# A two-block network on one core: order of the summed feed-forward products, and the gated recurrence with its two directions' scores added before they are multiplied

## The chip, the cores and the metric

The kernel runs on one core of a Trainium2 chip. A core has five engines that run their own instruction lists and meet at semaphores: TensorE (matrix products, PE in the rows, its weight loads PEld), VectorE (DVE), ScalarE (ACT), GpSimd (POOL) and SyncE (SP), which here only issues the weight transfers. The metric is the time of one execution on the device in microseconds (us); the time before is the median of three, 3287.19 us (3286.39 to 3287.36).

## The reference

Two blocks follow each other on 256 tokens of width 2048. The first has two layers, each a mixer and a convolved feed-forward part (`silu(gate) * val`, then `@ w_down`, 5632 by 2048). The mixer of layer 0 holds the gated recurrence, run forwards and backwards over segments of 64 tokens:

```python
def hgrn2_scan(q, k, v, log_f):
    ...
    scores = einsum('bhntd,bhnsd->bhnts', q * exp(b - b_mid), k * exp(b_mid - b))
    scores = where(mask, scores, 0.0)                 # mask: lower triangle of a segment
    o_intra = einsum('bhnts,bhnsv->bhntv', scores, v)
    kv = einsum('bhnsd,bhnsv->bhndv', k * exp(b_last - b), v)
    # S_{n+1} = exp(b_last) * S_n + kv_n
    o_inter = einsum('bhntd,bhndv->bhntv', q * exp(b), S_prev)
    return o_intra + o_inter

o_fw = hgrn2_scan(q, 1 - f_fw, i, log(f_fw))
o_bw = flip(hgrn2_scan(flip(q), flip(1 - f_bw), flip(i), flip(log(f_bw))))
o = rms_norm(o_fw + o_bw) * silu(g)
```

Both directions multiply their masked scores with the same `i`. The feed-forward down product is `hidden @ w_down` and the result goes through a residual sum and a layer norm.

## The kernel before

All large products are done in float32r as three products of a high and a low part: ScalarE copies a raw weight chunk of 128x2048 numbers into `w_hi` (`cast_chunk`, L320), VectorE writes the rest into `w_lo` (`split_chunk`, L324), and TensorE does hi by hi, hi by lo and lo by hi (L479, L480, L481). There are five raw buffers and three `w_hi` buffers: the cast of chunk n waits until TensorE has used chunk n-3, and SyncE fetches the raw chunk r when the user of raw chunk r-5 is done.

**The down stages** (`down0` from 949 us, `down1` from 1954 us of the profiled execution). Each has 55 steps in the order of `DOWN_STEPS`. A plain step, "chunk", is 24 matmuls of 128x128 by 128x512. Two by two blocks of the weights are multiplied in four groups by a scheme with seven products instead of eight, named by `DOWN_GROUP`: `b11`, `t1`, `t3`, `b22`, `p2`, `t4`, `t2`, of 12 matmuls each, with two or three plain chunks among them that fill the time. `t1`, `t2` and `t4` take sums of raw weights, which VectorE makes (`add`, L1064) in two `sums` buffers; `t1`, `t2`, `t3` and `b22` take sums of features ("mixed"), which `mix(j)` makes from eight VectorE instructions (L1046 to L1054), ScalarE casts (`mix_hi`, L1014) and VectorE splits (`mix_lo`, L1060). `mix(0)` serves the groups with j = 0, `mix(1)` those with j = 1. Steps 0 to 7 are plain, the first group begins at step 8, the second at step 18; `down_dve` writes VectorE's order by hand, `down_act` ScalarE's, and TensorE goes by `DOWN_STEPS`. In the groups with j = 1 VectorE also takes finished products out of the accumulators (`take_p1` L1081, `take_r5_r7` and `take_r6` L1083).

**The recurrence** (327 to 363 us). Heads are taken two at a time, in four rounds g. A round on TensorE is `hgrn_kv` (L1595, 12 matmuls), `hgrn_scores` (L1604, 8 matmuls) of the next round and `hgrn_values` of this one (L1617, 8 matmuls with the masked scores; L1622, 12 with the states). These are plain f32 matmuls, and the trace has two records for each. VectorE makes the states (`hgrn_states`: four copies L1528, eight steps L1530), masks the scores into zeroed memory (`hgrn_prob`, L1539), makes the queries (`hgrn_qdiff` L1508, `hgrn_qmid` L1516) and copies the result out (`hgrn_take`, L1578); ScalarE does the exponentials (L1473 to L1480) and the squares (L1491); GpSimd multiplies the queries (L1587). `hgrn_pe`, `hgrn_dve` and `hgrn_act` set the order by hand. After round 3, TensorE sums the squares (L1647) and goes on with the output product `mix0_out` (L479), whose third chunk waits for the normed result (L525).

## Time and profile before

| | |
|---|---|
| median of three runs | 3287.19 us |
| the profiled execution | 3286.53 us |
| its span, first to last instruction | 3284.7 us |
| TensorE busy | 3258.0 us (99%) |
| VectorE, ScalarE, GpSimd busy | 2389.6, 1447.5, 289.8 us |
| mean granted TensorE clock | 0.998 |
| transfers | 616 MB, 188 GB/s, the DMA engines about half busy |

Busy times of several engines overlap, so they don't add up; the span is the time of the chain that ended last, and a busy share says only how much of the span an engine had an instruction running. "PE busy" of 99% leaves 27 us of the span in which TensorE had none.

### The profile page before, as it was taken

The numbers are of one execution on the slowest core, as the hardware profiler recorded it, in microseconds if no ns is written. First come the engines' busy times: TensorE is split into PE (matmuls) and PEld (weight loads), VectorE is DVE, ScalarE is ACT, GpSimd is POOL, SyncE is SP. The second block draws the span as 40 slices with busy tenths as digits, with TensorE's granted clock in tenths as the row PEclk, the third lists the DMA queues.
The fourth block names the chain that finished last, engine by engine and source line by source line (L and its number), as shares of the span: only waits on it lengthen the run. The fifth ranks groups of instructions, "written<-read, shape, count | busy, mean of one in ns | idle before, by whom it ended". The sixth has DMA issues, their size and how long they took to land.

```text
span 3284.7 us, 40642 instructions
## 1 busy us (share of the span) xinstructions
PE 3258.0 (99%) x17302; PEld 2809.5 (86%) x17302; DVE 2389.6 (73%) x2310; ACT 1447.5 (44%) x1122; POOL 289.8 (9%) x108
## 2 busy tenths in 40 slices
PE   9999999999999999999999999999999999999999
PEld 8888888888888888888888887888888898888887
DVE  6756778888889886768888889888866566554554
ACT  6534443333335455644333334456633333355433
POOL 1300001111120000000111110000012011000000
PEclk9999999999999999999999999999999999999999
DMA  7554445555555465455555555545555544545554
GB/s 270 185 202 178 159 174 187 187 190 192 191 188 198 183 217 186 134 193 186 192 191 186 188 191 192 205 182 190 183 191 197 192 166 177 193 154 189 207 181 154
DMA packets 88306, 616.22 MB, mean 188 GB/s; under 512 B 10304, under 2 KB 11200, under 8 KB 15296
## 3 DMA queue, kind: packets, MB, share of 16 engines
q1 hardware_dynamic: 83232, 592.35, 50.1%
q10 hardware_dynamic: 4896, 21.30, 1.9%
q8 instruction: 136, 2.23, 0.3%
q14 instruction: 42, 0.34, 0.0%
HBM read 607.32 MB, written 2.10 MB: 186 GB/s over the span
## 4 chain that ended last, share of the span: by engine, by line
PE 94%; DVE 4%; DVEq 1%; ACT 1%; DMA 0%; issue 0%; SPq 0%; ACTq 0%
PE acc L407 53%; PE acc L479 6%; PE acc L480 6%; PE acc L481 6%; PE acc L433 6%; PE acc L431 6%; PE acc L432 6%; DVE w_lo L324 2%; PE acc L2158 0%; PE acc L1778 0%; PE acc L1842 0%; DVE over L1046 0%; DMA w_raw<-weights_dram 0%; PE acc L2262 0%; PE acc L515 0%; PE acc L2271 0%
## 5 line engine op out<-in xcount | busy, mean ns | idle before, releaser
L324 DVE TENSOR_TENSOR w_lo<-w_raw,w_hi 128x2048 fp32r<-128x2048 f32 x558 | 1354.6, 2431 | 626.7 <-ACT w_hi L320 623.5
L320 ACT ACTIVATE w_hi<-w_raw 128x2048 fp32r<-128x2048 f32 x558 | 1068.0, 1917 | 1459.5 <-PE acc L407 919.6
L407 PE MATMUL acc<-x_hi_lo,w_hi 128*128 128x512 f32 x5184 | 1212.8, 390 | 2.1 <-DVE w_lo L324 1.3
L407 PEld LDWEIGHTS acc<-x_hi_lo,w_hi 128*128 128x128 f32 x5184 | 960.9, 188 | 195.9 <-issue 4.2
L407 PEld LDWEIGHTS acc<-x_hi_lo,w_lo 128*128 128x128 f32 x5184 | 647.8, 191 | 16.8 <-DVE x_hi_lo L670 1.1
L407 PE MATMUL acc<-x_hi_lo,w_lo 128*128 128x256 f32 x5184 | 659.0, 284 | 1.2 <-DVE x_hi_lo L667 0.6
L431 PE MATMUL acc<-w_hi,x_hi_lo 128*128 128x512 f32 x736 | 288.2, 392 | 0.0
L433 PE MATMUL acc<-w_hi,x_hi_lo 128*128 128x512 f32 x736 | 286.5, 389 | 0.0
L432 PE MATMUL acc<-w_lo,x_hi_lo 128*128 128x512 f32 x736 | 286.4, 389 | 0.0
L479 PE MATMUL acc<-w_hi,hidden_hi_lo 128*128 128x512 f32 x672 | 264.2, 393 | 9.9 <-DVE w_lo L324 9.7
L481 PE MATMUL acc<-w_hi,hidden_hi_lo 128*128 128x512 f32 x672 | 262.8, 391 | 0.0
L480 PE MATMUL acc<-w_lo,hidden_hi_lo 128*128 128x512 f32 x640 | 250.3, 391 | 0.0
L856 DVE SCALAR_TENSOR_TENSOR over<-over,par,over 128x256 f32<-128x256 f32 x352 | 155.1, 482 | 13.5 <-issue 0.4
L433 PEld LDWEIGHTS acc<-w_hi,x_hi_lo 128*128 128x128 f32 x736 | 138.1, 188 | 29.0
L432 PEld LDWEIGHTS acc<-w_lo,x_hi_lo 128*128 128x128 f32 x736 | 138.2, 188 | 28.6
L479 PEld LDWEIGHTS acc<-w_hi,hidden_hi_lo 128*128 128x128 f32 x672 | 126.9, 189 | 41.3 <-issue 10.3
L431 PEld LDWEIGHTS acc<-w_hi,x_hi_lo 128*128 128x128 f32 x736 | 138.2, 188 | 28.0
L903 POOL TENSOR_TENSOR over<-over,over 128x1024 f32<-128x1024 f32 x22 | 56.6, 2572 | 1059.4 <-DVE over L856 1059.4
L481 PEld LDWEIGHTS acc<-w_hi,hidden_hi_lo 128*128 128x128 f32 x672 | 126.8, 189 | 26.5
L480 PEld LDWEIGHTS acc<-w_lo,hidden_hi_lo 128*128 128x128 f32 x640 | 121.0, 189 | 24.9
L499 DVE TENSOR_REDUCE over<-acc 128x256 f32<-128x512 f32 x176 | 109.0, 681 | 30.4 <-PE acc L407 30.4
L2301 POOL TENSOR_TENSOR over<-u_tiles,over 32x1024 f32<-32x1024 f32 x12 | 51.7, 4307 | 755.3 <-DVE u_tiles L499 755.3
(291 smaller groups left out, 2587.2 us busy)
## 6 DMA issues: line engine op xcount, KB each, us to landing
w_raw<-weights_dram SPq DMA_DIRECT2D x558, 1024.0 KB, 4.8
over<-rows_dram ACTq DMA_DIRECT2D x9, 1024.0 KB, 6.8
over<-over ACTq DMA_DIRECT2D x20, 128.0 KB, 2.4
u_tiles<-x_dram SPq DMA_DIRECT2D x4, 512.0 KB, 8.0
w_raw<-weights_dram SPq DMA_DIRECT2D x4, 512.0 KB, 7.0
resid<-x_tok_dram ACTq DMA_DIRECT2D x1, 2048.0 KB, 8.3
over<-w_gates_dram ACTq DMA_DIRECT2D x1, 2048.0 KB, 8.3
out_dram<-resid SPq DMA_DIRECT2D x8, 256.0 KB, 2.1
```

What stands on the lines that cost most here:

```text
L320: act.activation(whi[:, n % NHI, :], w_raw(n), ACT.Copy).then_inc(weights_hi, 1)
L324: dve.tensor_tensor(w_lo(n, 0, CHUNK), w_raw(n), whi[:, n % NHI, :].bitcast(F32), ALU.subtract).then_inc(weights_split, 1)
L407: last = pe.matmul(acc[:, 4 * t + f, 0:cols], weights, moving(k, 0, cols), start=(k == 0 and low == low_first), stop=(k == CK * nch - 1 an ...
L431: nc.tensor.matmul(dst, x_hi_b, hi, start=(k == 0), stop=False)
L432: nc.tensor.matmul(dst, x_hi_b, lo, start=False, stop=False)
L433: last = nc.tensor.matmul(dst, x_lo_b, hi, start=False, stop=(k == CK * nch - 1))
L479: nc.tensor.matmul(dst, x_hi_b, hi, start=first, stop=False)
L480: nc.tensor.matmul(dst, x_hi_b, lo, start=False, stop=False)
L481: return nc.tensor.matmul(dst, x_lo_b, hi, start=False, stop=last)
L499: return nc.vector.tensor_reduce(dst, halves(bank), AX, ALU.add)
L856: o = dve.scalar_tensor_tensor(out[:, f, :], pad[:, f, j:j + T], c(w0 + j * 2 * FT, f), out[:, f, :], ALU.mult, ALU.add)
L903: pool.tensor_tensor(vconv[:], vconv[:], gconv[:], ALU.mult)
```

## The change

Four things are done.

1. In `DOWN_GROUP` the last two entries are exchanged: `t2` comes before the plain chunk that closes a group. VectorE's order follows: all four splits of the group's end come before `take_r5_r7`, and the wait ahead of `finals(0, ...)` is on step `second - 1`.
2. In the down stages' first part, `mix(1)` is made after the splits of steps 6 and 7, not before the split of 6, and `mix_lo(1)` inside the first group, after the split of step 12. ScalarE's `mix_hi(1)` stands before the cast of 9, not of 7.
3. In the recurrence the masked scores of the two directions are added by VectorE (one more instruction of 128x512 in each round) and multiplied once: 4 matmuls with scores in a round, not 8. The masked scores lie in one buffer, the sums in two. A new semaphore, `scores_read`, lets TensorE make the next scores before the sum is there.
4. ScalarE copies the first states of rounds 1 to 3 (two instructions of 128x2x128, `hgrn_first_state`) and takes the results out of the accumulators (`hgrn_take`: a square and a copy of 128x512), which VectorE did with four copies and one. VectorE's `lo_part(2)` comes after the rounds.

```diff
-DOWN_GROUP = ("chunk", "b11", "t1", "chunk", "t3", "b22", "p2", "t4", "chunk", "t2")
+DOWN_GROUP = ("chunk", "b11", "t1", "chunk", "t3", "b22", "p2", "t4", "t2", "chunk")
@@ down_act
-            for i in range(3, 6):
-                cast(i)
-            mix_hi(0)
-            cast(6)
-            mix_hi(1)
-            for i in range(7, NDOWN - 1):
+            for i in range(3, NDOWN - 1):
+                if i == 6:
+                    mix_hi(0)
+                if i == 9:
+                    mix_hi(1)
                 cast(i)
@@ down_dve, group(p, j)
                 split(i0 + 4)
+                if (p, j) == (0, 0):
+                    mix_lo(1)
                 split(i0 + 5)
                 used(down_at(p, j, "t1"))
                 add(i0, t1, t2, held_raw(held, "b21"))
-                split(i0 + 6)
-                split(i0 + 7)
-                split(i0 + 8)
+                splits(i0 + 6, i0 + 10)
                 if j:
                     o = take_r5_r7(p)
                     if p == 0:
                         o.then_inc(shared_out, 1)
-                split(i0 + 9)
@@ down_dve
             mix(0)
             split(5)
             mix_lo(0)
+            splits(6, 8)
             mix(1)
-            split(6)
-            mix_lo(1)
-            split(7)
...
-            used(second - 2)
+            used(second - 1)
             finals(0, everything).then_inc(acc_free, 2)
@@ recurrence
+        def hgrn_first_state(act, g):
+            act.wait_ge(hg["kv_ps"], g + 1)
+            for dr in range(2):
...
+                o = act.activation(state[:, g % 2, 6 * dr:6 * dr + 4:3, :], kv, ACT.Copy)
+            o.then_inc(hg["first_state"], 1)
+        def hgrn_take(act, g):
+            act.wait_ge(hg["qcum"], g + 1)
+            act.wait_ge(hg["out_ps"], g + 1)
+            act.activation(flat(osq[:, 2 * g:2 * g + 2, :]), acc[:, 6 + g % 2, :], ACT.Square)
+            act.activation(flat(tiles(Q0 + 2 * g, 2)), acc[:, 6 + g % 2, :], ACT.Copy).then_inc(hg["out"], 1)
         def hgrn_act(act):
+            hgrn_first_state(act, 1)
             hi_part(act, 2, tiles(UU0))
             for g in range(2, NG):
                 hgrn_exps(act, g)
+                hgrn_take(act, g - 2)
+                hgrn_first_state(act, g)
             hgrn_in_act(7, 0, 1)
-            for b in range(4):
-                act.wait_ge(hg["out"], b + 1)
-                act.activation(osq[:, 2 * b:2 * b + 2, :], tiles(Q0 + 2 * b, 2), ACT.Square).then_inc(hg["sq"], 1)
+            for g in range(NG - 2, NG):
+                hgrn_take(act, g)
@@ hgrn_prob
-                o = dve.copy_predicated(prob[:, g % 2, 4 * dr:4 * dr + 4, :], mask[:].bitcast(I32),
+                o = dve.copy_predicated(masked[:, 4 * dr:4 * dr + 4, :], mask[:].bitcast(I32),
                                         acc[:, 4 + dr, :].rearrange("p (a n) -> p a n", a=4))
-            o.then_inc(hg["prob"], 1)
+            o.then_inc(hg["scores_read"], 1)
+            dve.drain()
+            dve.tensor_tensor(prob[:, g % 2], masked[:, 0:4, :], masked[:, 4:8, :], ALU.add).then_inc(hg["prob"], 1)
@@ hgrn_values
+                for b in range(2):
+                    pe.matmul(acc[:, bank, o0 + b * P:o0 + (b + 1) * P],
+                              i_block(b)[:, (2 * g + hh) * P:(2 * g + hh + 1) * P],
+                              prob[:, g % 2, 2 * hh + b, :], start=(b == 0), stop=False)
                 for a in (hh, 2 + hh):
-                    for b in range(2):
-                        pe.matmul(..., prob[:, g % 2, 2 * a + b, :], start=(a < 2 and b == 0), stop=False)
@@ hgrn_pe
-                    pe.wait_ge(hg["prob"], g + 1)
+                    pe.wait_ge(hg["scores_read"], g + 1)
                     hgrn_scores(pe, g + 1)
                 else:
                     pe.wait_ge(hg["state"], g + 1)
-                    pe.wait_ge(hg["prob"], g + 1)
+                pe.wait_ge(hg["prob"], g + 1)
                 hgrn_values(pe, g)
```

VectorE's order in `down0`, from the first feature sums to the third weight sum, before (L324 is a split, L1064 a weight sum, L1046 to L1054 a `mix`, L1060 a `mix_lo`):

```order
L1054 TENSOR_TENSOR over_74<-over_74 128x512
L324 TENSOR_TENSOR w_lo<-w_raw,w_hi 128x2048 [waits weights_hi]
L1060 TENSOR_TENSOR mixed_hi_lo<-over_74,mixed_hi_lo 128x2048 [waits mixed_hi]
L1046 TENSOR_TENSOR over_74<-hidden_hi_lo 128x1024 x2
L1049 TENSOR_TENSOR over_74<-over_74 128x512
L1050 TENSOR_TENSOR over_74<-over_74 128x512
L1052 TENSOR_TENSOR over_74<-over_74 128x512
L1054 TENSOR_TENSOR over_74<-over_74 128x512
L324 TENSOR_TENSOR w_lo<-w_raw,w_hi 128x2048 [waits weights_hi]
L1060 TENSOR_TENSOR mixed_hi_lo<-over_74,mixed_hi_lo 128x2048 [waits mixed_hi]
L324 TENSOR_TENSOR w_lo<-w_raw,w_hi 128x2048 [waits weights_hi]
```

The same place in the changed kernel, up to the second `mix_lo` (its lines are one lower):

```order
L1059 TENSOR_TENSOR mixed_hi_lo<-over_74,mixed_hi_lo 128x2048 [waits mixed_hi]
L324 TENSOR_TENSOR w_lo<-w_raw,w_hi 128x2048 [waits weights_hi] x2
L1045 TENSOR_TENSOR over_74<-hidden_hi_lo 128x1024 x2
L1048 TENSOR_TENSOR over_74<-over_74 128x512
...
L1053 TENSOR_TENSOR over_74<-over_74 128x512
L324 TENSOR_TENSOR w_lo<-w_raw,w_hi 128x2048 [waits weights_hi,hid_ready]
L1063 TENSOR_TENSOR over_71<-w_raw 128x2048 [waits raw_landed0,raw_landed4]
L324 TENSOR_TENSOR w_lo<-w_raw,w_hi 128x2048 [waits weights_hi]
L1063 TENSOR_TENSOR over_71<-over_71,w_raw 128x2048 [waits raw_landed1]
L324 TENSOR_TENSOR sums_lo<-over_71,w_hi 128x2048 [waits weights_hi]
L324 TENSOR_TENSOR w_lo<-w_raw,w_hi 128x2048 [waits weights_hi] x2
L1059 TENSOR_TENSOR mixed_hi_lo<-over_74,mixed_hi_lo 128x2048 [waits mixed_hi]
```

The splits of steps 6 and 7 have moved ahead of the second `mix`, and the second `mix_lo` behind the splits of steps 8 to 12.

VectorE's order at the end of the second group (steps 24 to 27 and after), before:

```order
L1064 TENSOR_TENSOR over_71<-over_71,w_raw 128x2048 [waits raw_landed0,chunk_used]
L324 TENSOR_TENSOR w_lo<-w_raw,w_hi 128x2048 [waits weights_hi]
L324 TENSOR_TENSOR sums_lo<-over_71,w_hi 128x2048 [waits weights_hi]
L1083 TENSOR_TENSOR resid<-resid,acc 128x512 [waits chunk_used]
L1083 TENSOR_TENSOR resid<-resid,acc 128x512 x3
L324 TENSOR_TENSOR sums_lo<-over_71,w_hi 128x2048 [waits weights_hi]
```

and in the changed kernel:

```order
L1063 TENSOR_TENSOR over_71<-over_71,w_raw 128x2048 [waits raw_landed0,chunk_used]
L324 TENSOR_TENSOR w_lo<-w_raw,w_hi 128x2048 [waits weights_hi]
L324 TENSOR_TENSOR sums_lo<-over_71,w_hi 128x2048 [waits weights_hi] x2
L1082 TENSOR_TENSOR resid<-resid,acc 128x512 [waits chunk_used]
L1082 TENSOR_TENSOR resid<-resid,acc 128x512 x3
```

The split of `t2` (the second `sums_lo`) follows that of `t4`, and the take-outs have moved behind all splits of the group.

VectorE's order in round 1 of the recurrence, before (the trailing queries are those of round 2):

```order
L1528 COPY over_86<-acc 128x128 [waits hg_kv_ps,hg_cumexp]
L1530 SCALAR_TENSOR_TENSOR over_86<-over_86,over_87,acc 128x128 x8
L1508 TENSOR_TENSOR over_85<-u_tiles 128x512 [waits hg_score_ps]
L1539 COPY_PREDICATED over_83<-over_90,acc 128x512 [waits hg_score_ps]
L1516 TENSOR_TENSOR over_85<-over_85,u_tiles 128x512 [waits hg_qexp]
L1578 COPY u_tiles<-acc 128x512 [waits hg_out_ps,hg_qcum]
L525 TENSOR_TENSOR x_hi_lo<-u_tiles,x_hi_lo 128x4x256 [waits x_hi]
```

and in the changed kernel, where the copies are ScalarE's:

```order
L1552 SCALAR_TENSOR_TENSOR over_87<-over_87,over_88,acc 128x128 [waits hg_first_state,hg_cumexp]
L1527 TENSOR_TENSOR over_86<-u_tiles 128x512 [waits hg_score_ps]
L1561 COPY_PREDICATED over_83<-over_91,acc 128x512 [waits hg_score_ps]
L1565 TENSOR_TENSOR over_84<-over_83 128x512
L1535 TENSOR_TENSOR over_86<-over_86,u_tiles 128x512 [waits hg_qexp]
```

The sum of the scores (L1565) now stands between the masking and the queries; the result's copy and the low part have left the round.

## Rows read from the trace of the kernel before

**Rows 1.** TensorE's waits, 940 to 1200 and 1960 to 2200: total us, times, longest

```profile
PE acc L479 <- DVE w_lo L324: 4.6, 3, 3.9
...
PE acc L479 <- DVE w_lo L324: 5.0, 4, 3.9
```

**Rows 2.** TensorE timeline, end of step 5 to step 7 of down0: start, duration, line

```profile
982.11 0.39 PE L481 MATMUL acc<-w_hi,hidden_hi_lo 128*128 128x512 f32 x1
986.38 0.47 PE L479 MATMUL acc<-w_hi,hidden_hi_lo 128*128 128x512 f32 x1 [3.89 <-DVE w_lo L324]
...
988.35 0.63 PE L480 MATMUL acc<-w_lo,hidden_hi_lo 128*128 128x512 f32 x1
...
993.51 0.39 PE L479 MATMUL acc<-w_hi,hidden_hi_lo 128*128 128x512 f32 x1
```

**Rows 3.** Windows: length, busy of PE, PEld, DVE, ACT, POOL, then PEclk, DMA share, GB/s

```profile
331.00:333.00 2.00, 0.44 (x4) 0.36 (x4) 1.76 (x5) 0.00 (x0) 0.00 (x0) 1.00 0.30 127
986.40:992.00 5.60, 5.60 (x18) 4.47 (x19) 5.60 (x3) 3.18 (x2) 0.00 (x0) 0.70 0.05 19
```

**Rows 4.** VectorE timeline, from the first `mix_lo` to the first weight sum

```profile
976.57 2.28 DVE L1060 TENSOR_TENSOR mixed_hi_lo<-over,mixed_hi_lo 128x2048 fp32r<-128x2048 f32 x1
978.77 2.35 DVE L1046 TENSOR_TENSOR over<-hidden_hi_lo 128x1024 f32<-128x1024 f32 x2
...
983.95 2.29 DVE L324 TENSOR_TENSOR w_lo<-w_raw,w_hi 128x2048 fp32r<-128x2048 f32 x1
...
988.36 4.49 DVE L324 TENSOR_TENSOR w_lo<-w_raw,w_hi 128x2048 fp32r<-128x2048 f32 x2
992.94 2.29 DVE L1064 TENSOR_TENSOR over<-w_raw 128x2048 f32<-128x2048 f32 x1
```

**Rows 5.** ScalarE timeline, casts of steps 3 and 4, released by steps 0 and 1

```profile
955.09 1.92 ACT L320 ACTIVATE w_hi<-w_raw 128x2048 fp32r<-128x2048 f32 x1 [3.52 <-PE acc L481]
960.53 1.92 ACT L320 ACTIVATE w_hi<-w_raw 128x2048 fp32r<-128x2048 f32 x1 [3.52 <-PE acc L481]
```

**Rows 6.** TensorE timeline, second group: into step 21, into step 24

```profile
1044.96 0.39 PE L481 MATMUL acc<-w_hi,mixed_hi_lo 128*128 128x512 f32 x1
1045.42 0.47 PE L479 MATMUL acc<-w_hi,hidden_hi_lo 128*128 128x512 f32 x1
...
1056.16 0.39 PE L481 MATMUL acc<-w_hi,mixed_hi_lo 128*128 128x512 f32 x1
1056.90 0.50 PE L479 MATMUL acc<-w_hi,hidden_hi_lo 128*128 128x512 f32 x1 [0.35 <-DVE w_lo L324]
```

**Rows 7.** VectorE timeline, the weight sum for t4 and the split of step 24

```profile
1052.35 2.29 DVE L1064 TENSOR_TENSOR over<-over,w_raw 128x2048 f32<-128x2048 f32 x1
1054.56 2.29 DVE L324 TENSOR_TENSOR w_lo<-w_raw,w_hi 128x2048 fp32r<-128x2048 f32 x1
```

**Rows 8.** TensorE timeline, starts of values 1, kv 3, scores 3, values 2

```profile
342.56 0.61 PE L1617 MATMUL acc<-over,u_tiles 128*128 128x128 f32 x4
...
347.07 1.71 PE L1595 MATMUL acc<-u_tiles 64*128 64x128 f32 x24
...
348.87 2.02 PE L1604 MATMUL acc<-over,u_tiles 128*128 128x128 f32 x16
...
350.73 0.61 PE L1617 MATMUL acc<-over,u_tiles 128*128 128x128 f32 x4
```

**Rows 9.** VectorE timeline, recurrence: queries 2, low part, states 2, queries 3

```profile
338.10 1.27 DVE L1516 TENSOR_TENSOR over<-over,u_tiles 128x512 f32<-128x512 f32 x2
...
339.90 1.98 DVE L525 TENSOR_TENSOR x_hi_lo<-u_tiles,x_hi_lo 128x1024 fp32r<-128x1024 f32 x1
...
342.75 2.32 DVE L1530 SCALAR_TENSOR_TENSOR over<-over,over,acc 128x128 f32<-128x128 f32 x8
...
347.43 1.29 DVE L1516 TENSOR_TENSOR over<-over,u_tiles 128x512 f32<-128x512 f32 x2
```

**Rows 10.** ScalarE groups: copies out of the accumulators, count, busy, mean ns

```profile
L2214 ACT ACTIVATE over<-acc 128x256 f32<-128x256 f32 x8 | 3.1, 390 | 0.0
```

38 lines of the change are left out of this document (18 added, 20 removed).

## The prediction

> **What bounds the kernel now.** I began with the table of busy times: TensorE is busy for 99% of the span, so the kernel can only gain by fewer or faster matmuls, or by closing the 27 us in which TensorE has none. What ScalarE or VectorE do counts only where TensorE waits for them. So the second view is TensorE's own waits, asked for stage by stage. In the two down stages they are almost all on VectorE's splits, and in each stage one wait has 3.9 us and the others share about a microsecond [rows 1]. The third view, the timeline there, shows two things [rows 2]. The last matmul of step 5 starts at 982.11 and the next one, which would have come 0.23 later, at 986.38: 4.04 lost. After that the matmuls take 0.63 where they took 0.39, and the 24 of step 6 last from 986.38 to 993.51, 7.13 us, where a plain step has 5.44 (two casts that successive steps release are 5.44 apart [rows 5]): another 1.69. The window there has a granted clock of 0.70, a mean of matmuls at 2.4 and at 1.2 GHz; a window in the recurrence with 0.44 us of matmuls in 2.00 has 1.00 [rows 3]. So the long wait is paid twice, 5.7 us in each stage, and waits of 1.6 us and less are paid once.
>
> What TensorE waits for is seen in VectorE's timeline [rows 4]: `mix_lo(0)` at 976.57, then all of `mix(1)` from 978.77 to 983.95, and only then the split of step 6, which ends at 986.24, 0.14 before TensorE goes on. Nothing before step 20 uses `mix(1)`.
>
> **The mixes (edit 2).** Removed: with `mix(1)` gone from there, the split of 6 can start at 978.77 and ends at 981.1, and TensorE wants it at 982.34. The cast of 6 is there, because it still follows `mix_hi(0)`. The cast of 7 now follows at once instead of after `mix_hi(1)`. So 4.04 and 1.69 go: 5.73 a stage, 11.5 in both. The longest wait of the second stage has the same 3.9 [rows 1].
>
> What is late next? I go on along VectorE. Two successive splits start 2.20 apart (988.36, two in 4.49), a sum behind a split starts 2.38 later [rows 4], and a split behind a sum 2.21 later [rows 7]; a `mix(1)` is 5.18 [rows 4]. From 978.77: splits 6 and 7; `mix(1)` from 983.17; split 8 at 988.35; sum at 990.73; split 9 at 992.94; sum; split 10 at 997.53; sum; split 11 at 1002.12, done 1004.41. TensorE from 982.34 with 5.44 for plain steps (6, 7, 8, 11) and 2.72 for the others: it wants 8 at 993.2 (ready at 990.6), 9 at 998.7, 10 at 1001.4 (ready 999.8), and 11 at 1004.10. So step 11 is late by 0.3 and, with the 0.1 from split to matmul, 0.4 to 0.5. Then split 12 at 1004.32, `mix_lo(1)` at 1006.52, split 13 at 1008.72, sum at 1011.10, split 14 at 1013.31, done 1015.60; TensorE, now 0.4 later, wants step 14 at 1015.4: late by 0.3. From there VectorE waits for ScalarE again and is ahead. Added: 0.75 a stage, 1.5 in all. Bounds: 0 if VectorE gets to its splits 0.5 sooner than I have it, and 1.9 a stage if it is a further microsecond late, which both waits would show. I take 0.75 because each of its durations has a row. Of ScalarE, `mix_hi(1)` (1.92) at 988.5 puts the cast of 9 at 990.3 to 992.2, just before VectorE wants it.
>
> **The order of a group (edit 1).** In the groups with j = 1 VectorE is behind, since it takes products out. TensorE starts step 21 0.46 after its predecessor instead of 0.23, and step 24 0.74 after, with the split of 24 ending at 1056.85 [rows 6, 7]; with the slower first matmul after each wait (1056.90 to 1057.24 is 0.1 too long) that is 0.3 and 0.6, 0.9 a group, four groups. VectorE is late there because the split of 19 has to wait for its cast, and that for step 16, which is plain and takes 5.44. Now 16 is `t2` and takes 2.72; VectorE starts the group about 0.85 sooner against TensorE, and both splits are in time by 0.1 or more. I count 0.75 a group, 3.0 in all; bounds 0 (if the slack of 0.1 is not there, and it only changes places) and 3.6. What gets tighter is the end of a group, `p2`, `t4`, `t2` of 2.72 each in a row. There the cast of n starts when n-3 is used, takes 1.92, the split 2.29, with some 0.3 between: 4.5 of the 5.44 that n-2 and n-1 last. Slack 0.9. The take-outs move behind the splits; `take_r5_r7` ends 2.2 to 3 later, and step 28, which waits for it, starts after the plain step 27: slack over 1. The raw chunk of step 21 is fetched into the buffer of step 17, not 16: freed 5.44 before its cast may start, and a fetch lands in 4.8 (the page's median over 558 fetches, in the section of DMA issues), so 0.6 is left, plus VectorE's own slack.
>
> **The recurrence (edits 3 and 4).** Removed: 4 matmuls, 8 records, in each of 4 rounds. A round of values has 40 records in 4.51 (342.56 to 347.07) [rows 8], 0.113 each, the 64 columns wide ones included; 32 fewer are 3.6 us, all on TensorE's path, for it had no wait of weight there but one of 1.6 at the first scores, which stays. But the queries now come behind the sum of scores on VectorE. In the trace queries 2 ran at 338.10 to 339.37 with kv 2 still before the scores that need them. Now they start 0.7 later, at 338.8, and end at 340.1, while TensorE, 0.9 ahead, wants them at 339.75: 0.45 late. GpSimd multiplies from 339.5, and beside it the low part took 1.98 for 1024 elements, 0.99 for 512, where the queries' product takes 0.64 [rows 9]; so 0.3 more. For round 2: the first states come from ScalarE at 341.3, after its exponentials, its take and two copies (0.39 each by the nearest row [rows 10]; instruction of two 128-blocks, not seen in the trace; 0.22, as VectorE's copies, to 0.6 bound it). VectorE: eight steps 2.3 [rows 9], differences 1.2, masks 1.3, sum 0.7, queries 1.3: done at 348.1. From 342.75 to 347.43 the first three of these took 4.68 [rows 9], the sum of my parts. TensorE wants the queries at 347.3 (values 1 from 342.1 to 345.65, kv 1.64): 0.85 late. The last round's sum is late by 0.1. Together 1.7 of waits; ends: 0.8 (no GpSimd effect, ScalarE's copies at the fast end) and 3.0 (copies at the slow end, every queries product at 0.99). 3.6 - 1.7 leaves 1.9, plus 0.1 for a small gap that the waits swallow: 2.0. The tail (squares, norm, the wait for the low part) shifts with it: ScalarE takes square and copy in 1.2 after the last values, where copy and square on two engines took 1.6.
>
> One thing in rows speaks against this part. Short waits did not lower the clock: 1.00 in the window that holds 1.6 without a matmul [rows 3]. The Trainium skill (TensorE: Matmul & The Clock Gate, section "A second HAM failure mode: psum-queue depth-cycling") tells of a kernel in which frequent very short idle times between groups of matmuls made the clock swing between its two levels. By that rule the recurrence, with four waits now, could run slow; the trace has one wait there and does not show it. It is the third rival below.
>
> **The sum.** 11.5 - 1.5 + 3.0 + 2.0 = 15.0. The profiled execution took 3286.5, 0.7 under the median of 3287.2; its time becomes 3271.5 and the median 3272.2. I take 3272.
>
> **Rivals.**
> 1. *VectorE is later in the first group than I have it.* The mixed sums beside anything that slows them; a wait at step 11 that grows to about 4 us brings the low clock with it. For it: `mix(0)`, beside GpSimd, took 8.3 where `mix(1)` took 5.2. Against: GpSimd is done by 970.5, and its column is 0.00 in the window behind [rows 3]. Three microseconds more in each stage, 3 + 1.7 = 4.7 twice: 3281.5. Half of it, without the clock, 3275.
> 2. *The end of a group turns into a wait.* If the weights land 1.5 later than the median, or the take-outs hold the accumulators, TensorE waits 1 us in each of the eight groups and edit 1 gains nothing: 3272 + 3 + 8 = 3283, at most. For it: slacks of 0.6 to 0.9 are small. Against: `b22`, `p2`, `t4` already ran as a row of short steps without a wait in the groups with j = 0.
> 3. *Slower.* TensorE falls to 1.2 GHz at the queries' waits of the recurrence and stays there until the dense output product has run for a while. Place: from scores 2 (340.2) to the squares' end (360.4), 20 us, of which 18.5 are matmuls. At half the clock a matmul of 512 columns took 0.63 - 0.20 = 0.43 to the next instead of 0.23 [rows 2]; by that factor 1.9 the stage takes 16.5 longer, and 1.7 more after it: 3272 + 18 = 3290. It decides from about 15 us at the low level. Against: the full clock in the 1.6 wait, longer than any I expect.
> 4. *The recurrence gives nothing* (waits of 3.6): 3274.
>
> **How the numbers follow.** My forecast with its own spread (3269 to 3275, from the bounds: recurrence 0.6 to 2.8, added waits 0 to 3.8, groups 0 to 3.6, small gaps I did not count) has 0.70, with rival 4 inside it. Rival 1 in its halves 0.13, rival 2 0.08, rival 3 0.03, and 0.06 for more gain than all this, when the shorter waits that I hold to stay go too. The range 3267.5 to 3277.5 leaves out the full sizes of 1 to 3. From one kernel to another 0.2%, 6.6 us, can be told from no change: faster is below 3280.6. Of rival 1 and 2 about 0.07 lie above, most of it within 0.2%: faster 0.91, same 0.06, slower 0.03.
>
> **What would show it.** Right: no wait of more than 1 us in the down stages, granted clock 1.00 at 982 to 994 and its like; two short waits, of `b11`'s next plain step and of `p2` in the first group of each stage; none in the second groups; 64 records of the scores' product down to 32, and waits before scores 2 and 3 in the recurrence of 0.5 to 1.1. Wrong: a window under 1.00 anywhere in the three stages, waits at `t4`, `t2` or behind them, or a recurrence from the first values (334.5) to the squares (359.6) that lasts over 24 us.

## The result, and the profile after

| | before | after |
|---|---|---|
| median (6 runs each) | 3287.17 us (3286.39 to 3287.62) | 3269.44 us (3269.01 to 3269.54) |
| ratio of the two | | 0.9946, 95% interval 0.9933 to 0.9959 |
| the profiled execution | 3286.53 us | 3269.4 us |
| its span | 3284.7 us | 3267.3 us |

Forecast were 3272.0 us and a range of 3267.5 to 3277.5. The kernel gained 17.7 us where 15.0 was forecast.

**Where the time went.** I cut both traces at the same matmuls (the first of each product after a stage) and took the time between the cuts:

| stretch | before | after | change |
|---|---|---|---|
| start to the end of mix0_out, with the recurrence | 451.28 | 448.14 | -3.14 |
| first up stage | 498.11 | 498.11 | 0 |
| down0 | 236.47 | 229.77 | -6.70 |
| attention | 269.82 | 269.82 | 0 |
| second up stage | 498.11 | 498.10 | 0 |
| down1 | 237.31 | 229.75 | -7.56 |
| the rest of the span | 1093.60 | 1093.61 | 0 |

The changes add to 17.4, the difference of the spans. Nothing was given back in the stages between. The first stretch is good to about 0.3 only: among five kernels that are the same up to the down stages it ends between 450.94 and 451.28, nearly all of it because the first scores start between 332.36 and 332.67. Counted from the first scores, the gain is 3.02, and the other 0.12 lies ahead of them.

**The down stages.** TensorE's waits from 940 to 1200 and from 1960 to 2200; each row has the engine and line that waited, the releaser, then us in total, times, and the longest:

```profile
PE acc L479 <- DVE w_lo L324: 0.3, 1, 0.3
...
PE acc L479 <- DVE w_lo L324: 0.3, 1, 0.3
```

These answer to [rows 1]: 4.6 and 5.0 with a longest wait of 3.9 have become 0.3 and 0.3.

TensorE's timeline goes through the place where it had stood still, then into step 11 and into step 14 (start, duration, line):

```profile
982.14 0.39 PE L480 MATMUL acc<-w_lo,hidden_hi_lo 128*128 128x512 f32 x1
982.37 0.39 PE L481 MATMUL acc<-w_hi,hidden_hi_lo 128*128 128x512 f32 x1
...
1000.73 0.39 PE L481 MATMUL acc<-w_hi,mixed_hi_lo 128*128 128x512 f32 x1
1001.39 0.47 PE L479 MATMUL acc<-w_hi,hidden_hi_lo 128*128 128x512 f32 x1 [0.28 <-DVE w_lo L324]
...
1012.14 0.39 PE L481 MATMUL acc<-w_hi,mixed_hi_lo 128*128 128x512 f32 x1
1012.50 0.50 PE L479 MATMUL acc<-w_hi,hidden_hi_lo 128*128 128x512 f32 x1
```

Against [rows 2], the matmuls now follow each other at 0.23 without a break and take 0.39, not 0.63. Step 6 takes 5.44, before 7.13. The matmuls at 1001.39 and 1012.50 start 0.66 and 0.36 after the one ahead of them instead of 0.23. These are the two short waits that were forecast, at step 11 and at step 14. There is no third in the whole first group, and the second groups, where [rows 6] had two, have none.

The windows (length, busy of PE, PEld, DVE, ACT, POOL, then PEclk, DMA share, GB/s) for the same stretch and for the recurrence:

```profile
982.00:994.00 12.00, 12.00 (x55) 9.93 (x54) 11.59 (x9) 5.65 (x3) 0.00 (x0) 1.00 0.58 214
...
325.00:360.00 35.00, 32.61 (x284) 29.48 (x282) 26.16 (x51) 17.73 (x30) 6.06 (x4) 1.00 0.17 60
```

The granted clock, 0.70 in [rows 3], is 1.00. It is 1.00 in the recurrence too, with its new waits.

VectorE's timeline from the splits of steps 6 and 7 on:

```profile
975.63 4.49 DVE L324 TENSOR_TENSOR w_lo<-w_raw,w_hi 128x2048 fp32r<-128x2048 f32 x2
980.03 2.35 DVE L1045 TENSOR_TENSOR over<-hidden_hi_lo 128x1024 f32<-128x1024 f32 x2
...
985.21 2.28 DVE L324 TENSOR_TENSOR w_lo<-w_raw,w_hi 128x2048 fp32r<-128x2048 f32 x1
987.58 2.29 DVE L1063 TENSOR_TENSOR over<-w_raw 128x2048 f32<-128x2048 f32 x1
989.79 2.28 DVE L324 TENSOR_TENSOR w_lo<-w_raw,w_hi 128x2048 fp32r<-128x2048 f32 x1
```

Here [rows 4] had `mix(1)` at 978.77, right behind `mix_lo(0)`, and the split of 6 behind it. Now the splits of 6 and 7 come first and `mix(1)` follows at 980.03. Take off the 3.14 by which the stage starts sooner, and the forecast had the split of 8 at 985.21, the sum at 987.59 and the split of 9 at 989.80. The rows have 985.21, 987.58 and 989.79: a timeline worked out from neighbouring durations can be that good.

**The recurrence.** TensorE's waits from 300 to 420, and its timeline from the first scores to the output product:

```profile
PE acc L1619 <- issue: 1.6, 1, 1.6
PE acc L1619 <- DVE over L1535: 0.8, 2, 0.5
PE acc L479 <- DVE x_hi_lo L525: 0.6, 1, 0.6
```

```profile
332.55 2.02 PE L1619 MATMUL acc<-over,u_tiles 128*128 128x128 f32 x16 [1.56 <-issue]
...
340.07 2.02 PE L1619 MATMUL acc<-over,u_tiles 128*128 128x128 f32 x16 [0.34 <-DVE over L1535]
341.93 0.61 PE L1631 MATMUL acc<-over,u_tiles 128*128 128x128 f32 x4
...
345.54 1.71 PE L1610 MATMUL acc<-u_tiles 64*128 64x128 f32 x24
347.74 2.02 PE L1619 MATMUL acc<-over,u_tiles 128*128 128x128 f32 x16 [0.48 <-DVE over L1535]
...
359.78 0.79 PE L479 MATMUL acc<-w_hi,x_hi_lo 128*128 128x512 f32 x1
```

Values 1 run from 341.93 to the next kv at 345.54, 3.61, where [rows 8] had 4.51 from 342.56 to 347.07: 0.90 a round and 3.6 in four. The cost is two waits for the queries, 0.34 before scores 2 and 0.48 before scores 3. From the first scores (332.55) to the output product (359.78) it is 27.2, before 30.0 (332.67 to 362.70), so the recurrence is 2.8 shorter, and 0.2 to 0.3 more came at the output product's last chunk, where the wait for the low part (L525) fell from 0.8 to 0.6.

VectorE's timeline, round 2, with the instructions that I had to bound:

```profile
338.03 0.69 DVE L1565 TENSOR_TENSOR over<-over 128x512 f32<-128x512 f32 x1
338.64 1.29 DVE L1535 TENSOR_TENSOR over<-over,u_tiles 128x512 f32<-128x512 f32 x2
340.80 2.32 DVE L1552 SCALAR_TENSOR_TENSOR over<-over,over,acc 128x128 f32<-128x128 f32 x8 [0.88 <-ACT over L1490]
```

The queries (L1535) took 1.29 for two, as in [rows 9] without GpSimd, although GpSimd started its own products at 339.26 (the last section shows what GpSimd does to VectorE and what it doesn't). The last row shows a wait that costs TensorE nothing by itself: VectorE stands 0.88 for ScalarE's first states, in round 3 again 0.87. The experiments come back to it. ScalarE takes a result in each of these rounds and then copies the first states:

```profile
340.04 0.66 ACT L1490 ACTIVATE over<-acc 128x256 f32<-128x256 f32 x2
```

The two copies of first states took 0.66 together, 0.33 each; 0.39 was assumed, between 0.22 and 0.6.

### The profile page after: what moved, and what is told of

Its sections match the earlier page's. It is cut to its first block, busy times and chain, and to the rows that moved or that the text cites. A ratio compares the mean times of both kernels' runs of the same rounds, so it can differ in the third digit from the quotient of the medians.

```text
span 3267.3 us, 40580 instructions
## 1 busy us (share of the span) xinstructions
PE 3249.2 (99%) x17270; PEld 2803.9 (86%) x17270; DVE 2385.4 (73%) x2298; ACT 1451.0 (44%) x1132; POOL 289.1 (9%) x108
## 4 chain that ended last, share of the span: by engine, by line
PE 93%; DVE 4%; DVEq 1%; ACT 1%; DMA 0%; issue 0%; SPq 0%; ACTq 0%
PE acc L407 54%; PE acc L479 6%; PE acc L481 6%; PE acc L480 6%; PE acc L431 6%; PE acc L432 6%; PE acc L433 6%; DVE w_lo L324 1%; DVEq L1062 1%; PE acc L2173 0%; PE acc L1793 0%; PE acc L1857 0%; DVE over L1045 0%; DMA w_raw<-weights_dram 0%; PE acc L2277 0%; PE acc L515 0%
## 5 line engine op out<-in xcount | busy, mean ns | idle before, releaser
L324 DVE TENSOR_TENSOR w_lo<-w_raw,w_hi 128x2048 fp32r<-128x2048 f32 x558 | 1354.2, 2430 | 623.8 <-ACT w_hi L320 620.4
```

The lines of the kernel that those rows point to most:

```text
L324: dve.tensor_tensor(w_lo(n, 0, CHUNK), w_raw(n), whi[:, n % NHI, :].bitcast(F32), ALU.subtract).then_inc(weights_split, 1)
```

## The experiments

Each kernel was profiled once and timed 4 to 10 times beside the kernel before, which had medians of 3287.19, 3287.23 and 3287.3 us in the three groups of runs; times of different groups can be compared to about 0.1. The last three columns give the time between the cuts used above.

| | median us | ratio to before (95%) | start to mix0_out | down0 | down1 |
|---|---|---|---|---|---|
| before | 3287.17 | | 451.28 | 236.47 | 237.31 |
| after | 3269.44 | 0.9946 (0.9933 to 0.9959) | 448.14 | 229.77 | 229.75 |
| edit 2 alone | 3276.47 | 0.9968 (0.9956 to 0.9981) | 450.94 | 231.48 | 232.35 |
| edit 1 alone | 3282.38 | 0.9987 (0.9977 to 0.9996) | 451.0 | 234.76 | 235.68 |
| edits 3 and 4 alone | 3284.5 | 0.999 (0.998 to 1.0) | 448.24 | 237.31 | 237.25 |
| before, gap filled | 3283.09 | 0.9989 (0.9979 to 0.9998) | 451.0 | 234.79 | 235.64 |
| before, gap half filled | 3284.81 | 0.9993 (0.9984 to 1.0003) | 451.2 | 234.85 | 237.27 |
| edit 3 alone | 3288.74 | 1.0005 (0.9996 to 1.0015) | 453.57 | 237.32 | 237.26 |
| edit 4 alone | 3287.24 | 1.0001 (0.9991 to 1.0011) | 450.83 | 236.44 | 237.43 |
| after, queries first | 3269.26 | 0.9946 (0.993 to 0.9963) | 447.9 | 229.78 | 229.82 |
| after, mixes later | 3270.3 | 0.9949 (0.9933 to 0.9966) | 448.06 | 230.22 | 230.21 |
| after, queries and first states first | 3268.69 | 0.9944 (0.993 to 0.9957) | 447.11 | 229.77 | 229.78 |

### Edit 2 alone: the mixes

```diff
 (kernel before)
@@ down_act
-            for i in range(3, 6):
-                cast(i)
-            mix_hi(0)
-            cast(6)
-            mix_hi(1)
-            for i in range(7, NDOWN - 1):
+            for i in range(3, NDOWN - 1):
+                if i == 6:
+                    mix_hi(0)
+                if i == 9:
+                    mix_hi(1)
                 cast(i)
@@ down_dve: mix(1) after splits 6 and 7, mix_lo(1) after the split of 12
```

> Edit 2 alone (the mixes behind the splits of steps 6 and 7) on the kernel before. My theory: the 3.9 us wait ahead of step 6 and the slow matmuls behind it go (5.7 us a stage), and waits of 0.6 us at step 11 and 0.2 at step 14 come (0.8 with the slower first matmuls), while the waits at steps 21 and 24 of the groups with j = 1 and the one at the end of down1 stay: 2 x 4.9 less, 3277.3. Rival (the gain needs the group's new order too, because VectorE hands its delay on to the second group): waits at steps 21 and 24 grow by the delay and the time is 3280 or more.

Measured: 3276.47, 10.7 less. Both down stages lost 4.99 and 4.96: the 5.73 that the long wait and the low clock cost, less 0.7 of new waits. TensorE's waits from 940 to 1200, and its way into steps 21 and 24:

```profile
PE acc L479 <- DVE w_lo L324: 1.0, 3, 0.4
...
1039.67 0.39 PE L481 MATMUL acc<-w_hi,mixed_hi_lo 128*128 128x512 f32 x1
1040.12 0.47 PE L479 MATMUL acc<-w_hi,hidden_hi_lo 128*128 128x512 f32 x1
...
1050.89 0.39 PE L481 MATMUL acc<-w_hi,mixed_hi_lo 128*128 128x512 f32 x1
1051.60 0.50 PE L479 MATMUL acc<-w_hi,hidden_hi_lo 128*128 128x512 f32 x1 [0.32 <-DVE w_lo L324]
```

The long wait is gone, and the pair of [rows 6] is still there: 0.45 and 0.71 from start to start where they were 0.46 and 0.74. So the mixes have nothing to do with the waits in the second groups, and edit 1's gain is its own.

### Edit 1 alone: the order of a group

```diff
 (kernel before)
-DOWN_GROUP = (..., "p2", "t4", "chunk", "t2")
+DOWN_GROUP = (..., "p2", "t4", "t2", "chunk")
@@ group(p, j): four splits in a row, then take_r5_r7
-                split(i0 + 6)
-                split(i0 + 7)
-                split(i0 + 8)
+                splits(i0 + 6, i0 + 10)
...
-                split(i0 + 9)
@@
-            used(second - 2)
+            used(second - 1)
```

> Edit 1 alone (t2 ahead of the plain step that closes a group) on the kernel before. My theory: the waits at steps 21, 24, 45 and 48 go (1.85 us a stage), and the wait of 0.65 (0.8 with the slower first matmul) ahead of the last step of down1 goes, since take_r6 then doesn't wait for t2: 4.5 less in all, 3282.7; the 3.9 us waits stay. Rival (the last step's wait in down1 went for another reason, the mixes' or the recurrence's): it is still there and the time is 3283.5.

Measured: 3282.38, 4.8 less. In down0, where step 6 took 7.17 (before 7.13), the two groups with j = 1 gave 1.71 together, 0.85 each. In down1 only 1.63 shows, but step 6 took 8.10 there, 0.93 more than before. Without that it would be 2.56, 0.8 or more above the two groups' share. The rest is a wait that the forecast did not have. In the kernel before, TensorE's timeline goes into the last step of down1, and VectorE's shows where the time went. (The steps are counted from 0 and the last is 55; there are 56 of them, not the 55 given above.)

```profile
2179.16 0.39 PE L481 MATMUL acc<-w_hi,hidden_hi_lo 128*128 128x512 f32 x1
2180.04 0.50 PE L479 MATMUL acc<-w_hi,hidden_hi_lo 128*128 128x512 f32 x1 [0.50 <-DVE w_lo L324]
```

```profile
2168.77 1.89 DVE L1083 TENSOR_TENSOR resid<-resid,acc 128x512 f32<-128x512 f32 x3 [2.53 <-PE acc L481]
```

`take_r6(1)` has to wait until TensorE has used the last `t2`. With `t2` in the last place of the group VectorE stood 2.53 for it, and the remaining splits came late: the last step began 0.88 after its predecessor's last matmul, not 0.23. With edit 1, `t2` is done 5.44 earlier. In the kernel after, the same take waits for nothing:

```profile
2150.59 1.88 DVE L1082 TENSOR_TENSOR resid<-resid,acc 128x512 f32<-128x512 f32 x3
```

All six kernels without edit 1 that were run beside the kernel before still have a step of 0.88 or 0.89 there; the kernel with edit 1 alone has 0.23.

TensorE never had this wait in down0, but not because VectorE was better off there: it stood 2.50 for the same product. Its split of the last step comes at the same place in both stages, 223.93 after the start of down0 (949.39) and 223.92 after that of down1 (1953.79).

What differs is when TensorE asks for it. At the end of a stage it does the first 128 tokens of the last steps in a row and then the second 128, and `NHELD = {"down0": 2, "down1": 3}` says for how many steps. With three, it wants the last weights half a plain step, 2.72, sooner: 225.6 after the start instead of 228.3, where the split ends at 226.2. No run changed `NHELD`; this is read from the code and the rows.

### Edits 3 and 4 alone: the recurrence

```diff
 (kernel after)
@@ the down stages as in the kernel before (edits 1 and 2 undone)
```

> Edits 3 and 4 alone (summed scores, ScalarE with first states and results) on the kernel before. My theory: 3.1 us less, all before the output product, 3284.1, with waits of 0.34 and 0.48 before scores 2 and 3. Rival (a part of it is given back when the output product then waits for weights or the norm): under 2 us less, 3285.2 or more.

Measured: 3284.5, 2.7 less; the stretch with the recurrence lost 3.04, as in the kernel after (3.14). The three runs add to 10.7 + 4.8 + 2.7 = 18.2 where all together gave 17.7. With intervals of about 0.1% (3.3 us) each, that is no sign that the edits act on each other. The stretches are sharper: 9.95 in the down stages for edit 2, 4.3 for edit 1 with step 6 of equal length, and 3.0 in the recurrence make 17.3, against 17.4 together. In this profile step 6 of down0 took 7.99 instead of 7.13, which is all of the 0.84 by which its down0 is longer than before's.

### The gap filled

```diff
 (kernel before)
@@ TensorE, ahead of step 6 of each down stage
+                if i == 6:
+                    pe.wait_ge(acc_free, TASK0[name] + 2)
+                    for _ in range(16):
+                        pe.matmul(acc[:, 7, 0:P], ones[:], ones[:], start=True, stop=True)
```

The products go to a place that is overwritten before it is read.

> The kernel before with 16 matmuls of ones (128x128 f32, 0.23 us each, 3.6 us in all) in the gap ahead of step 6 of each down stage, into an accumulator that nobody uses then; the wait for the split of 6 stays. My theory: the granted clock stays at 1.00 and the 24 matmuls of step 6 take 5.5 us instead of 7.1, 1.7 less a stage: 3283.8. Rival (the matmuls behind the wait are slow for another reason, VectorE or the transfers): 3287.2, window still under 1.00.

Measured: 3283.09, 4.1 less, with 32 more records on TensorE in each stage. Its timeline into step 6, and the window of step 6:

```profile
982.04 3.73 PE L983 MATMUL acc<-ones 128*128 128x128 f32 x32
985.98 0.50 PE L479 MATMUL acc<-w_hi,hidden_hi_lo 128*128 128x512 f32 x1 [0.21 <-DVE w_lo L324]
```

```profile
986.40:992.00 5.60, 5.60 (x26) 4.62 (x25) 5.60 (x3) 3.07 (x3) 0.00 (x0) 1.00 0.01 3
```

The split comes no sooner, and step 6 starts as late as before. But the window has clock 1.00 instead of the 0.70 of [rows 3], with 26 matmuls instead of 18, and step 6 takes 5.57 and 5.61 in the two stages. So the second part of the penalty is the clock's and comes of the empty gap, not of the late split. By the profiles it was worth 1.68 in down0 and 1.67 in down1; by the medians 4.1 for both, 0.7 more. The likely reason is that the low clock does not always cost as much (the last section), and that the profile of before has both of its stretches in the cheap form. The single runs speak for it: of the six of before, two lie at 3286.39 and 3286.64 and four at 3287.15 to 3287.62, and the profiled one, at 3286.53, is of the lower kind.

### The gap half filled

```diff
-                    for _ in range(16):
+                    for _ in range(8):
```

> The kernel before with 8 small matmuls of ones by ones (128 columns, f32) between steps 5 and 6 of each down stage; their product is overwritten. 16 of them in the same place kept the clock up. The wait on the split of 6 stays, and TensorE now has about 2.0 us with matmuls and 2.0 without in a gap of 4. Theory (what matters is how long TensorE has nothing in one piece, and 1.6 us is short enough): step 6 takes 5.5 to 5.6, and the time is that of the run with 16, 3283.1 (3282.6 to 3284.0). Rival (a gap that is half empty is as bad as an empty one, as the 2.7 us wait in the recurrence with summed scores alone was followed by slow matmuls): step 6 takes 7.1 to 8.1, and the time stays within 0.7 of 3287.2.

Measured: 3284.81, from 3283.3 to 3286.44, between the two theories, and the profile has both. TensorE's timeline into step 6 of down0 and of down1:

```profile
982.28 1.95 PE L983 MATMUL acc<-ones 128*128 128x128 f32 x16
986.19 0.50 PE L479 MATMUL acc<-w_hi,hidden_hi_lo 128*128 128x512 f32 x1 [1.97 <-DVE w_lo L324]
...
1985.06 1.95 PE L983 MATMUL acc<-ones 128*128 128x128 f32 x16
1988.99 0.64 PE L479 MATMUL acc<-w_hi,hidden_hi_lo 128*128 128x512 f32 x1 [1.98 <-DVE w_lo L324]
1989.43 0.63 PE L480 MATMUL acc<-w_lo,hidden_hi_lo 128*128 128x512 f32 x1
```

The same gap, with the same 1.95 of matmuls and then 1.97 or 1.98 of nothing, was followed by full speed (0.40) in one stage and by the lower level (0.63) in the other. Neither theory holds as I wrote it: at this size of wait it is sometimes one, sometimes the other, in one execution. The ten runs say the same: one at 3283.3, six at 3284.5 to 3284.9, three at 3286.2 to 3286.4.

### Edit 3 alone: summed scores, VectorE copies all

```diff
 (kernel before)
@@ hgrn_prob: masked scores in one buffer, their sum in two; scores_read, then
+            dve.tensor_tensor(prob[:, g % 2], masked[:, 0:4, :], masked[:, 4:8, :], ALU.add).then_inc(hg["prob"], 1)
@@ hgrn_values: 4 matmuls with scores, not 8
@@ first states and results stay with VectorE
```

> Edit 3 alone (the summed scores) on the kernel before; VectorE keeps the copies of first states and results. My theory: VectorE's round grows by the sum of 0.7 us and TensorE waits for the queries ahead of scores 3 by about 2.7 us, 0.4 ahead of scores 2 and 0.5 for the last sum, so that the 3.6 us of matmuls are given back: no more than 0.3 faster than before, 3286.9 to 3287.4. Rival (the matmuls count by themselves): 3284.

Measured: 3288.74, and the stretch with the recurrence 2.3 longer than before, though TensorE has 32 records less. That was outside both expectations. TensorE's timeline at scores 2 and scores 3, and the window behind:

```profile
341.12 2.02 PE L1606 MATMUL acc<-over,u_tiles 128*128 128x128 f32 x16 [1.29 <-DVE over L1516]
...
350.98 2.60 PE L1606 MATMUL acc<-over,u_tiles 128*128 128x128 f32 x16 [2.67 <-DVE over L1516]
```

```profile
350.00:355.00 5.00, 4.03 (x25) 4.05 (x25) 4.85 (x16) 3.48 (x5) 3.01 (x2) 0.72 0.01 3
```

VectorE is the bound of every round: to steps, differences, masks and queries come four copies (0.87), a copy of the result (0.69) and the new sum (0.69), and once, ahead of scores 3, the low part (1.70), which edit 4 moves behind the rounds. TensorE waits 1.29 and then 2.67 for the queries, and behind the second wait the clock falls: 0.72 in the window, and the 16 records of scores 3 last 2.60 instead of 2.02. From the start of scores 3 to the second half of values 2 it is 5.22, in the kernel after 3.59, so 1.6 of the 2.3 are the clock's, and without it the waits would have cost 0.7 more than the saved matmuls gave. My forecast had the long wait right, took 0.4 for the one of 1.29, and left out the clock. This is the mechanism of rival 3, in a small form; the kernel after, with waits of 0.34 and 0.48, shows none of it.

### Edit 4 alone: ScalarE takes results and first states

```diff
 (kernel after, edits 1 and 2 undone)
@@ hgrn_prob, hgrn_values, hgrn_pe as in the kernel before
```

> Edit 4 alone (ScalarE with first states and results) on the kernel before; both directions' scores are multiplied as before. My theory: TensorE had only 0.25 us of waits for VectorE in the recurrence, and 0.2 in the tail, so 0.3 to 0.5 less: 3286.8. Rival (the shorter VectorE round is itself the gain): 3284 or 3285.

Measured: 3287.24; the stretch with the recurrence 0.45 shorter, 0.34 from the first scores on. VectorE is relieved, but it was hardly what TensorE waited for, and TensorE keeps all its matmuls. So edit 3 alone loses 2.3, edit 4 alone gives 0.3 to 0.45, and both together give 3.0 to 3.1. Edit 4's worth is that it frees on VectorE the time that edit 3's sum takes there.

The median doesn't show even the 0.45. One reason lies outside the span: the whole time is 1.7 to 1.9 us longer than the span in the runs of the kernels without edit 4, and 1.9 to 2.1 in those with it, 0.2 more on average. No run shows where that 0.2 is spent, but it comes off what edit 4 gains.

### After, with the queries ahead of the sum

```diff
 (kernel after)
@@ VectorE, each round
                 hgrn_prob(dve, g)          # masks only
                 if g + 1 < NG:
                     hgrn_qmid(dve, g + 1)
+                hgrn_sum(dve, g)
```

> The changed kernel with VectorE's sum of the masked scores behind the next round's queries, not ahead of them. My theory: the two waits before scores 2 and 3 (0.34 and 0.48 in the profile, 0.95 with the slower first matmuls) go and the sum is still in time for the values: 3268.5. Rival (the waits are ScalarE's, by the first states it delivers): they stay, 3269.4.

Measured: 3269.26, 0.2 below the kernel after, with ranges that overlap (3269.14 to 3269.4 against 3269.01 to 3269.54); the stretch with the recurrence 0.24 shorter, 0.16 from the first scores on. Both waits of the kernel after are gone, as expected, but their 0.8 is not: TensorE gets ahead and waits elsewhere, as its timeline and then VectorE's show.

```profile
352.86 0.68 PE L1635 MATMUL acc<-over,u_tiles 128*128 128x128 f32 x4 [0.49 <-issue]
```

```profile
348.39 2.32 DVE L1552 SCALAR_TENSOR_TENSOR over<-over,over,acc 128x128 f32<-128x128 f32 x8 [0.92 <-ACT over L1490]
...
352.06 0.69 DVE L1567 TENSOR_TENSOR over<-over 128x512 f32<-128x512 f32 x1
```

The profile names nobody for the wait at values 3, but the sum that they need ends at 352.75, 0.11 before they start. Going back from it: masks, eight steps of states from 348.39, and ahead of those 0.92 in which VectorE waits for ScalarE's first states. The bound is then not the order on VectorE alone but the loop of VectorE (differences), ScalarE (exponentials, take, first states) and VectorE again.

### After, with first states ahead of the take as well

```diff
 (kernel with the queries ahead of the sum)
@@ hgrn_act
                 hgrn_exps(act, g)
-                hgrn_take(act, g - 2)
-                hgrn_first_state(act, g)
+                hgrn_first_state(act, g)
+                hgrn_take(act, g - 2)
```

> The changed kernel with two exchanges in the recurrence: VectorE makes the queries of the next round before the sum of the scores, and ScalarE copies the first states before it takes the result of the round before. With the first exchange alone TensorE's waits before scores 2 and 3 went (0.34 and 0.48), but it waited 0.49 at values 3 for the sum, whose chain hung 0.9 us a round on ScalarE's first states. Theory (that chain is the bound): the states come 1.17 earlier, VectorE has no wait of 0.9 at L1552 any more, the wait at values 3 goes, the recurrence is 0.5 to 0.9 shorter than with the first exchange alone, 3268.4 to 3268.9 in all. Rival (TensorE's lead is given back behind the recurrence, at the output product's last chunk, which waits for norm and low part on ScalarE and VectorE): the three waits go and the one at the output product grows by the same, 3269.1 to 3269.5.

Measured: 3268.69 (3268.36 to 3268.93), below every run of the kernel after (3269.01 to 3269.54), and the stretch with the recurrence 0.79 shorter than with the first exchange alone, 1.03 shorter than after (0.74 and 0.90 from the first scores on). TensorE's waits from 300 to 420:

```profile
PE acc L1623 <- issue: 1.6, 1, 1.6
PE acc L479 <- DVE x_hi_lo L525: 0.6, 1, 0.6
```

Behind the first scores (1.6, as ever) no wait is left in the rounds, and the one behind them is as it was, so the rival is refuted: the output product starts at 358.74 instead of 359.78, and it all arrives. VectorE's waits for first states did not go, as I had written, but fell:

```profile
340.40 2.32 DVE L1552 SCALAR_TENSOR_TENSOR over<-over,over,acc 128x128 f32<-128x128 f32 x8 [0.63 <-ACT over L1490]
...
347.54 2.32 DVE L1552 SCALAR_TENSOR_TENSOR over<-over,over,acc 128x128 f32<-128x128 f32 x8 [0.40 <-ACT over L1490]
```

What is left of them comes from TensorE: ScalarE's copies at 339.64 have themselves waited 0.59 for the kv.

This version beats both kernels, by 0.75 us over the one after: two exchanges in the order.

### After, with the mixes one split later

```diff
 (kernel after)
-            splits(3, 5)
+            splits(3, 6)
             dve.wait_ge(chunk_used, n0)
             mix(0)
-            split(5)
+            split(6)
             mix_lo(0)
-            splits(6, 8)
+            split(7)
             mix(1)
@@ ScalarE: mix_hi(0) ahead of the cast of 7, not of 6
```

> The changed kernel with every step of the mixes behind one more split in the down stages: VectorE does splits 3, 4, 5, mix(0), split 6, mix_lo(0), split 7, mix(1), and ScalarE's mix_hi(0) follows the cast of 6. My theory: the split of 5 is in time (0.2 us), mix(0) runs mostly after GpSimd has finished and takes under 6.5 us, not 8.3, and VectorE is a microsecond ahead in the first group, so that the waits at steps 5, 11 and 14 go: 1.0 a stage, 3267.4. Rival (VectorE is bound by its work there and the lateness only moves to another step): 3269.4.

Measured: 3270.3, 0.9 slower than after, 0.45 in each down stage, so the rival was right. VectorE's timeline, and TensorE's into step 11:

```profile
964.70 3.98 DVE L324 TENSOR_TENSOR w_lo<-w_raw,w_hi 128x2048 fp32r<-128x2048 f32 x1 [1.73 <-ACT w_hi L320]
...
985.55 2.29 DVE L324 TENSOR_TENSOR w_lo<-w_raw,w_hi 128x2048 fp32r<-128x2048 f32 x1
```

```profile
1001.74 0.47 PE L479 MATMUL acc<-w_hi,hidden_hi_lo 128*128 128x512 f32 x1 [1.01 <-DVE w_lo L324]
```

Before and after, step 5 had begun 0.43 after the matmul ahead of it, 0.2 too late. That went, and `mix(0)`, now clear of GpSimd, took 5.2 instead of 8.3. But the split of 5 in its stead took 3.98 beside GpSimd, with 1.73 of waiting for the cast ahead of it. The split of 8 starts at 985.55 instead of 985.21, TensorE begins step 8 at 989.69 instead of 990.08, and step 11 waits 1.01 instead of 0.28 (1.39 from start to start instead of 0.66). The lateness was VectorE's, and it only moved.

## Why the prediction was right, and where it was off

**The mixes: 11.5 forecast.** The step held. The long wait is gone in both stages, the clock stays at its upper level, and the filled gap shows that the 1.69 was really the clock's. By the profiles the part that edit 2 removes is the 5.73 a stage that stood in the forecast: down0 lost 4.99 with edit 2 alone, and its two new waits cost 0.72. The median gained more than the profile: the profiled execution of before lay 0.7 under its median because both low stretches in it were short ones. I had carried that 0.7 on as a constant. By that reading it belonged to the part that was removed, and so is gain: the kernel after has its profiled execution at its median (3269.4, 3269.44).

**New waits: 1.5 forecast, 1.5 measured.** Step 11 lost 0.43 (0.66 less 0.23), forecast about 0.45; step 14 lost 0.13, forecast 0.3; the matmul behind each wait is slower and costs another 0.08 and 0.11, which the forecast had in neither term. Together 0.75 a stage: two small errors cancel here.

**The groups: 3.0 forecast, 3.4 measured.** Edit 1 alone gave 0.85 a group in down0. I had read 0.9 and written off 0.15 of it as restart, without need. The forecast's slacks at the end of a group were enough: no wait at `t4`, `t2` or the chunk behind them. Whether the fetch of step 21 has the 0.6 to spare that I gave it, no run tried.

**The term that was missing: 0.8.** I followed the step of [rows 6] through two groups and doubled it. But the two stages of [rows 1] are not alike: 5.0 in four waits against 4.6 in three. The fourth was the one at the last step of down1. It hung on `t2`, the very product that edit 1 moves, and it showed in down1 alone because `NHELD` is 3 there and 2 in down0. To ask what differs between two stages that should be alike would have found it.

**The recurrence: 2.0 forecast, 3.1 measured.** The removed part was right (3.6). The waits were mis-sized: I had 1.7 and they are 0.34 + 0.48 + about 0.15 for restarts, 1.0. Of the 0.7 too much, 0.3 was "GpSimd multiplies beside it": I took the low part's 0.99 for 512 elements and put it on another instruction of the same engine; the queries product took 0.64 beside GpSimd as without. The low part had started behind GpSimd and was held up; the queries start ahead of it (the last section). Round 3's wait, 0.85 forecast, was 0.48; the first states came 0.06 a copy faster than I had them, and the last round's sum made no wait at all. The rest is 0.2 at the wait for the low part in the output product and the 0.1 ahead of the first scores.

**The sum**, from the spans: 11.5 - 1.5 + 3.4 + 0.8 + 3.1 = 17.3, against 17.4. The forecast of 3272 lay 2.6 over the result: 1.1 in the recurrence, 0.8 in the missing wait, 0.4 in the groups and 0.6 or 0.7 in what was carried on from the profiled execution, less 0.2 to 0.3 that edit 4 adds outside the span. That the range held is in part luck: the new waits were right by two errors that cancel, and the others, which all but the last point one way, were small enough together.

**The rivals.** Rival 1, VectorE later in the first group: no; its timeline came out within 0.02 up to the split of step 14. But the last experiment shows how near it is, since a VectorE 0.34 later and a TensorE 0.39 earlier turned the wait of 0.28 into one of 1.01. Rival 2, waits at the end of a group: none. Rival 4, a recurrence that gives nothing: no. Rival 3, a low clock in the recurrence: not in the kernel after (1.00 from 325 to 360). The rule that I weighed there (the Trainium skill, TensorE: Matmul & The Clock Gate, section "A second HAM failure mode: psum-queue depth-cycling", on frequent very short idle times) does not show in this kernel with its four waits, of 1.6, 0.3, 0.5 and 0.6 us. With edit 3 alone the clock did fall, behind a wait of 2.67 that followed one of 1.29.

## What to carry to other kernels

A wait of TensorE is worth more than its length once it is long enough to lower the clock: read the steps behind it and not only the wait, and fix the longest single wait before many short ones. When work moves from one engine to another to relieve a third, judge the parts together: here the summed scores cost 2.3 us alone, the relieved VectorE gave 0.45 at most, and both gave 3.1. And when a stage runs twice, compare its two sets of waits first; the one wait that only one of them has is a term that doubling misses. Look for the reason in the engine that asks as well as in the one that delivers: here VectorE did the same in both stages, and TensorE asked sooner in one.

## What the runs showed of the hardware that was not expected

**The low clock costs a varying time.** Behind a wait of 3.9 us, step 6 (5.44 at full clock) took 7.13 and 7.17 us before, 7.17 and 8.10 with edit 1 alone, 7.99 and 7.16 with edits 3 and 4 alone, 8.02 and 7.12 with edit 3 alone, 7.15 and 6.93 with edit 4 alone: 1.5 to 1.7 more in seven stages of ten, 2.6 or 2.7 more in three. The low level doesn't always begin with the end of the wait. In down0 of before four more ran at full speed and the low level came 1.3 us after the first; in the three costlier stages, and in the one of 6.93, it was there already when the matmuls came back. The varying length is probably most of why the kernels with the wait scatter (3286.39 to 3287.62 before, 3281.78 to 3283.06 with edit 1 alone) and those without hardly do (3269.01 to 3269.54 after, 3282.99 to 3283.29 with the gap filled).

**Whether it comes at all varies too, near 2 us.** After waits of 1.56 (in the recurrence of before) and less the records show full clock; after 2.67 (with one of 1.29 ahead of it) and 3.9 the lower level; after 1.97 full clock and after 1.98, in the same execution, the lower level for eight matmuls.

**Of GpSimd and VectorE, the one that started second stood still.** In the kernel after, VectorE's split of step 4 and GpSimd's product ahead of it are:

```profile
959.34 3.71 DVE L324 TENSOR_TENSOR w_lo<-w_raw,w_hi 128x2048 fp32r<-128x2048 f32 x1 [0.70 <-ACT w_hi L320]
```

```profile
956.58 4.32 POOL L903 TENSOR_TENSOR over<-over,over 128x1024 f32<-128x1024 f32 x1 [33.92 <-DVE over L856]
```

The split of step 3 (956.35 to 958.64) had started 0.23 before GpSimd and kept its 2.29; GpSimd's product took 4.32 and ended 2.26 after the split (960.90 against 958.64). The same product took 2.40 in the turn before, at 914.54, where it had started first. The split of step 4 started while GpSimd was at work, and ended 2.15 after it (963.05). With the mixes one split later the split of 5 took 3.98 and again ended 2.15 after GpSimd; the two mixed sums (1.2 each alone) took 2.05 and 3.46, and each ended 1.08 after. VectorE's second queries product in the recurrence kept its time (0.69 by itself, 1.29 for the two) where it had started 0.02 before GpSimd's, which took 1.80 there instead of 1.27. The steps of the states (L1552), which take one operand from the accumulators, took 0.34 or 0.35 beside GpSimd as without. So for these instructions the order of start decides who pays, and what looks like a slow instruction is a wait that the trace books as busy time.
